# Hybrid decoder trunk on one core: the last weight unit of every expert layer packed by column halves, the output combined between the halves, and TensorE's branch placed at a fixed slot of a fetch block

## The reference, cut to what matters

```python
for layer in range(4):
    kind = layer % 3                     # 0 forgetting attention, 1 HGRN2, 2 short convolution
    mixed = (forgetting_attention, hgrn2, short_conv)[kind](x, ...)
    x = layer_norm(DEEPNORM_ALPHA * x + mixed, ln_mix_g[layer], ln_mix_b[layer])
    # 4 groups of 8 experts: the best group of each token, the two best experts in it
    gates = ...                          # (256 tokens, 32 experts), two non-zero values a token
    hg, hu = jnp.einsum('btd,edf->btef', x, w_gate), jnp.einsum('btd,edf->btef', x, w_up)
    h = jax.nn.silu(hg) * hu * gates[..., None]
    ffn = jnp.einsum('btef,efd->btd', h, w_down)
    x = layer_norm(DEEPNORM_ALPHA * x + ffn, ln_ffn_g[layer], ln_ffn_b[layer])
```

## Time and profile before

| | |
|---|---|
| median of 3 runs | 1457.16 us (1450.97 to 1460.29) |
| the profiled execution's own time | 1457.11 us |
| its span, first to last instruction | 1455.2 us |
| TensorE busy (matmuls / weight loads) | 90% / 50% of the span |
| VectorE, ScalarE, GpSimd busy | 25%, 21%, 7% |
| moved by DMA | 482 MB, 331 GB/s over the span |
| TensorE's mean granted clock | 0.987 of full speed |

### The profile page before, as it was taken

How to read it: one execution, slowest core, us unless ns; L and a number is a source line. 1 busy time by engine, 2 the same in 40 slices (tenths; PEclk the granted TensorE clock), 3 DMA queues, 4 the chain that set the end, 5 groups by cost and what they waited for, 6 DMA issues and landing times.

```text
span 1455.2 us, 18373 instructions
## 1 busy us (share of the span) xinstructions
PE 1308.8 (90%) x7662; PEld 734.2 (50%) x7662; DVE 364.8 (25%) x928; ACT 305.8 (21%) x751; POOL 96.4 (7%) x170
## 2 busy tenths in 40 slices
PE   8999988878999999888789999889789999888885
PEld 7855633422564865343328866333328765543331
DVE  1442311102615843111111133110112451311103
ACT  0241312112223312222111003221110251312210
POOL 2221000000001520000000000000001030000000
PEclk9999999999999999999999999999999999999998
DMA  9756699999735029999998837999998355899995
GB/s 320 278 225 274 257 427 429 426 427 415 311 122 225 2 84 422 429 426 429 427 427 355 370 144 275 428 427 427 428 417 360 118 231 235 331 428 426 429 426 212
DMA packets 36773, 481.97 MB, mean 331 GB/s; under 512 B 4416, under 2 KB 4736, under 8 KB 6864
## 3 DMA queue, kind: packets, MB, share of 16 engines
q1 hardware_dynamic: 35424, 478.19, 79.7%
q0 software_dynamic: 1120, 2.09, 0.7%
q10 hardware_dynamic: 144, 0.46, 0.1%
HBM read 479.60 MB, written 1.05 MB: 330 GB/s over the span
## 4 chain that ended last, share of the span: by engine, by line
PE 75%; DMA 13%; DVE 5%; ACT 4%; issue 2%; POOL 1%; SPq 0%; DVEq 0%; POOLq 0%
PE psum L785 15%; DMA memory<-in_units 13%; PE psum L1085 12%; PE psum L816 8%; PE psum L1045 8%; PE psum L844 8%; PE psum L1128 7%; PE psum L1120 7%; ACT memory L1224 2%; PE psum L824 1%; DVE memory L1912 1%; PE psum L1181 1%; ACT memory L1420 1%; PE psum L750 1%; PE psum L958 1%
## 5 line engine op out<-in xcount | busy, mean ns | idle before, releaser
L785 PE MATMUL psum<-memory,ring 128*128 128x256 f32 x1024 | 224.1, 382 | 1.5 <-DMA ring<-in_units 1.1
L785 PEld LDWEIGHTS psum<-memory,ring 128*128 128x128 f32 x1024 | 195.6, 191 | 29.0 <-issue 1.3
L1128 PE MATMUL psum<-memory 128*128 128x512 f32 x256 | 128.5, 628 | 42.8 <-DVE memory L1912 22.8
L1045 PE MATMUL psum<-memory,x 128*128 128x128 f32 x1024 | 130.6, 281 | 35.0 <-ACT memory L1224 35.0
L1045 PEld LDWEIGHTS psum<-memory,x 128*128 128x128 f32 x1024 | 119.3, 192 | 72.9 <-issue 69.9
L1085 PE MATMUL psum<-ring,memory 128*32 128x512 f32 x1152 | 136.2, 612 | 14.2 <-DMA ring<-in_units 14.0
L1224 ACT ACTIVATE memory<-psum,affine_t 128x128 f32<-128x128 f32 x312 | 117.3, 457 | 136.9 <-PE psum L1045 129.4
L1907 DVE TENSOR_TENSOR memory<-memory,psum 128x256 f32<-128x256 f32 x32 | 13.5, 421 | 461.9 <-ACT memory L1414 461.9
L844 PE MATMUL psum<-ring,memory 128*128 128x512 f32 x256 | 112.4, 594 | 1.4 <-DVE memory L1501 0.9
L1128 PEld LDWEIGHTS psum<-memory 128*128 128x128 f32 x256 | 44.7, 193 | 131.9 <-DVE memory L1912 48.2
L1085 PE MATMUL psum<-memory 128*32 128x512 f32 x896 | 103.5, 602 | 5.6 <-DMA memory<-in_units 5.5
(11 more groups left out here) (222 smaller groups left out, 1147.5 us busy)
## 6 DMA issues: line engine op xcount, KB each, us to landing
ring<-in_units SPq DMA_DIRECT2D x129, 2048.0 KB, 25.4
memory<-in_units SPq DMA_DIRECT2D x88, 2048.0 KB, 26.3
memory<-in_units SPq DMA_DIRECT2D x16, 1024.0 KB, 27.4
ring<-in_units SPq DMA_DIRECT2D x4, 512.0 KB, 10.5
memory<-in_const SPq DMA_DIRECT2D x3, 448.0 KB, 31.2
x<-in_x SPq DMA_DIRECT2D x2, 512.0 KB, 4.8
out<-x SPq DMA_DIRECT2D x2, 512.0 KB, 2.7
memory<-in_tables SPq DMA_DIRECT2D x1, 640.0 KB, 31.4
```

The costliest lines, as they stand in the source:

```text
L785: last = nc.tensor.matmul(bank(key, T, s * T), w[:, 2 * m + s, k, :], xT[:, k, :], start=(k == 0), stop=(k == KD - 1))
L1045: last = nc.tensor.matmul(psum[:, to, (at + i) * P:(at + i + 1) * P], x[:, c, k * P:(k + 1) * P], sel[:, par, c, :], start=(c == 0), stop= ...
L1128: last = nc.tensor.matmul(psum[:, 4 + NH * c + h, :], hT[:, FC + c, :], y_sb[:, h * HB:(h + 1) * HB], start=False, stop=last_quad, skip_gr ...
```

## The change

1. Packing: a second copy of each layer's last unit is added behind the others, laid out by output columns: columns 512 to 767 for both j first, then columns 768 to 1023. The last unit is loaded from this copy, in the same two DMAs of 1 MB.
2. `down(1)` of a last quad becomes `down_columns(0)` and `down_columns(1)`, of 256 columns each over both j, into bank 3 and bank 1. Each is eight matmuls, where each j of `down(1)` was four.
3. `combine(0)` moves between them, ahead of the wait on the second DMA. `combine(1)` becomes `combine_columns(0)` and `combine_columns(1)`, of 256 columns each; `z_ready` comes from the second.
4. ScalarE copies the two banks separately (128x256 each), the first once `columns_used` tells that `down_columns(0)` is done.
5. TensorE's flag read gets an alignment: it is put at slot 128 of a block of 256 instruction slots, and a branch leads over the padding.

```diff
+                    at = PACKED + unit[1]
                     for j in range(FC):
                         cols = slice(j * UNIT // FC, (j + 1) * UNIT // FC)
...
-                        if j and h == NH - 1 and last_quad and sems is first:
-                            pe.wait_ge(half_in, 16 * (n // NQ + 1))
...
-                if last_quad:
+                half = HB // 2
+                def down_columns(b):
+                    w = slots[GU + 1][0].rearrange("p (b j e c) -> p b e j c", b=2, e=QE, j=FC)
+                    for j in range(FC):
+                        for e in range(QE):
+                            rows = slice(W * e, W * (e + 1))
+                            last = nc.tensor.matmul(psum[rows, (3, 1)[b], 0:half], hT[:, j, rows], w[:, b, e, j],
+                                                    start=(j == 0), stop=(j == FC - 1))
+                    return last
+
+                def combine_columns(b):
+                    cols = slice(b * half, (b + 1) * half)
+                    return [nc.tensor.matmul(psum[:, 4 + NH * c + 1, cols], hT[:, FC + c, :], y_sb[:, HB:D][:, cols],
+                                             start=False, stop=True, skip_group_check=True) for c in range(TC)]
+
+                if last_quad and sems is first:
+                    l = n // NQ
+                    down(0)
+                    pe.wait_ge(*slots[GU + 1][1])
+                    down_columns(0).then_inc(columns_used, 1)
+                    combine(0)
+                    pe.wait_ge(half_in, 16 * (l + 1))
+                    down_columns(1).then_inc(sems["unit_used"], 1)
+                    pe.wait_ge(columns_ready, l + 1)
+                    combine_columns(0)
+                    pe.wait_ge(sems["y1_ready"], n + (1 + FREE))
+                    for last in combine_columns(1):
+                        last.then_inc(z_ready, 1)
+                elif last_quad:
...
                 experts(l)
+
+                pe.addr_align(256, offset=128, max_nops=0)
                 runs = more_path(pe, l, runs, experts_more)
...
+                if by_columns:
+                    act.wait_ge(columns_used, l + 1)
+                    nc.scalar.activation(y_sb[:, HB:HB + HB // 2], psum[:, 3, 0:HB // 2], ACT.Copy).then_inc(columns_ready, 1)
+                    act.wait_ge(sems["unit_used"], n * QU + QU)
+                    nc.scalar.activation(y_sb[:, HB + HB // 2:D], psum[:, 1, 0:HB // 2], ACT.Copy).then_inc(sems["y1_ready"], 1)
...
-    units = np.empty((PACKED, P, UNIT), np.float32)
+    units = np.empty((PACKED + DEPTH, P, UNIT), np.float32)
...
+        units[PACKED + l] = moe[-1, -1].reshape(P, FC, QE, 2, HB // 2).transpose(0, 3, 1, 2, 4).reshape(P, UNIT)
```

More of the change, by code:

```diff
@@ L428, in build @@
         unit_used, half_ready = sem("unit_used"), sem("half_ready")
+        columns_used, columns_ready = sem("columns_used"), sem("columns_ready")
         pair_gathered, pair_ready = sem("pair_gathered"), sem("pair_ready")
@@ L1129, in combine @@
                                                 start=False, stop=last_quad, skip_group_check=True)
-                        if last_quad and sems is first and h == NH - 1:
-                            last.then_inc(z_ready, 1)
                     if last_quad and sems is first and h == 0:
@@ L1409, in first_tokens, with quad @@
                 token_blocks(l, 0, (2, 3), 2).then_inc(first["xw_ready"], 1)
-            def quad(l, sems, n, par, ahead):
+            def quad(l, sems, n, par, ahead, by_columns=False):
                 act.wait_ge(sems["unit_used"], n * QU + (GU + spare(sems)))
@@ L1417, in quad @@
                     tokens(l, sems, n + 1, 1 - par, 1)
-                act.wait_ge(sems["unit_used"], n * QU + (QU + spare(sems)))
-                nc.scalar.activation(y_sb[:, HB:D], psum[:, 3, :], ACT.Copy).then_inc(sems["y1_ready"], 1)
+                if by_columns:
[3 more added lines that the diff above has]
+                    nc.scalar.activation(y_sb[:, HB + HB // 2:D], psum[:, 1, 0:HB // 2], ACT.Copy).then_inc(sems["y1_ready"], 1)
+                else:
+                    act.wait_ge(sems["unit_used"], n * QU + (QU + spare(sems)))
+                    nc.scalar.activation(y_sb[:, HB:D], psum[:, 3, :], ACT.Copy).then_inc(sems["y1_ready"], 1)
             def experts(l):
@@ L1428, in experts @@
                 for par in range(2):
-                    quad(l, first, l * NQ + NQ - 2 + par, par, par == 0)
+                    quad(l, first, l * NQ + NQ - 2 + par, par, par == 0, par == 1)
             def experts_more(l, runs):
```

## The result

Twelve runs of each: 1465.39 us median after (1461.18 to 1467.63), 1455.55 before (1450.97 to 1460.29). Ratio 1.0063, 95% interval 1.0051 to 1.0075 (the two medians alone give 1.0068). The profiled execution took 1461.18 us with a span of 1459.4; it is the fastest of its twelve, so it shows less of the loss (4.1 us) than the medians (9.8).

The account below looks back on a forecast made before the run. The weight stream was taken to bound the four expert ends, where matmuls wait for the last unit. 1457.11 us less 7.0 of gain plus 0.9 for the branch gave 1451.0 us, range 1445 to 1462.

Parts of the forecast that it names:

- the price of the branch: TensorE's branch after the flag read, layers 1 and 2: waits for a missing instruction block, 0.9 us lost together.
- the lower price: Branch in layers 1 and 2: transfer starts at once on landing, costing 0.4 and 0.5 us.
- The 2.46 us: Layer 1 of the kernel before: an instruction block is usable some 2.46 us after its transfer begins.
- The upper bound, 6.3: Branch in layers 1 and 2: transfer starts 4 us after landing, TensorE resumes 6.3 us after landing.
- L: Each layer's expert end: start of the first matmul of the last unit's second half, which waited for its DMA.
- the upper price: Branch in layers 1 and 2: late transfer, keep_busy at half clock, 5 us lost in each against before.
- the second case: Rival, chance 0.30: the branch over two blocks stalls TensorE in layers 1 and 2, sum 1457 to 1462 us.
- 5.1 us of gain in layers 0 and 3: Expert ends of layers 0 and 3: gains of 2.5 and 2.6 us, set against the stall's losses.
- The sum from L to the statistics: Expert ends: work before VectorE's first statistics on the second 512 columns falls to 2.66 us; layer 1 had 4.30.
- The cover before L: DMA wait in the expert ends: combine(0), 1.72 us, fits in layers 0 and 3, ends late in 1 and 2.
- My 7.0: Four expert ends: gains of 2.5, 0.5, 1.4 and 2.6 us, sum 7.0 us, bounds 5.2 and 8.3.
- Does the rest follow?: Stages behind the statistics: the gain is handed on whole; with a full stream, only layer 3's 2 to 3 us.

Follow-up runs that it names:

- columns_far: Changed kernel with the flag read aligned to slot 240 instead of 128 in layers 1 and 2: 1466.83 us, ratio 1.0089 to the kernel before.
- columns_only: Changed kernel without the alignment of the flag read: 1450.82 us, ratio 0.9967 to the kernel before.
- rows_between: Kernel before with only combine(0) moved between the two row halves of down(1), no column halves, no alignment: 1450.05 us, ratio 0.9975.
- align_only: Kernel before with only the alignment of the flag read to slot 128 added: 1455.40 us, ratio 1.0003.
- after_again: Changed kernel, unedited, measured again on the chip of three other runs: 1466.10 us, ratio 1.0081 to the kernel before.
- rows_overshoot: Kernel before, no column halves, flag read aligned to slots 128, 88, 80, 128 so layers 1 and 2 overshoot: 1467.54 us, ratio 1.0081.
- columns_fit: Changed kernel with the flag read aligned to slots 128, 160, 208, 128 of layers 0 to 3: 1459.61 us, ratio 1.0030 to the kernel before.
- busy_first: Changed kernel with the three keep_busy matmuls between padding and flag read instead of behind the branch: 1457.22 us, ratio 1.0022 to the kernel before.
- columns_unmoved: Column halves without alignment, combine(0) left behind both halves (edited from columns_only): 1456.22 us, ratio 1.0011 to the kernel before.
- early_overshoot: columns_only with an overshooting padding at the start of the last quads of layers 1 and 2: 1450.31 us, ratio 0.9975 to the kernel before.
- columns_busy_first: columns_only with the three keep_busy matmuls ahead of the flag read: 1448.85 us, ratio 0.9959 to the kernel before.

## Why the prediction was wrong

Forecast 1451.0 us in 1445 to 1462, measured 1465.39.

**The step that failed** is the price of the branch: "I take the lower price, the one that rows measure." The 2.46 us were the time from a transfer's start to its use, and the sum took the transfer to start with the landing. It started 3.3 us after it in layer 1 and 3.6 in layer 2; landing to use was 6.1 and 6.4 us by the same reckoning. The upper bound, 6.3, was the right value, and the trace before had the row for it: the branches of its layers 1 and 2 jump into a block too, and the next transfer begins 3.8 and 3.9 us after they end. Here is the first of the two transfers, in the 0.2 us from 765.6; its branch had ended at 761.93:

```profile
q8 instruction: 1, 0.02, 31.8%
```

The forecast used such a pass as no more than an upper end. The choice between the ends was made by the row that measured one piece of the wait, not the whole.

There is a row that speaks for a quick start, and the forecast didn't use it either. In layers 1 and 2 of the kernel before, the sequencer runs into a block in order, 17 and 13 slots ahead of the flag read by the count and so behind the wait at L; the next transfer began there at most 1.5 and 1.4 us after L (at 759.47 and 1084.57). In layer 2 of columns_far, 20 slots ahead, it began 3.3 us after L. So 3.3 us isn't what every entry costs under the stream; in all landings in a new block by a jump under it, in all kernels, it was 3.1 to 4.4. What sets the difference no run here shows.

**The case itself was right.** The slot count held in every layer: overshoot in 1 and 2, none in 0. It held for the further kernels too: each branch of over 2 us stood where the target's block was missing by the count, those of layer 3 among them, and none stood elsewhere. `keep_busy` at half clock behind the wait, estimated at 4.3 us, took 4.4 and 5.1. But with the upper price the second case read 1462, and the measurement is 3 us past that. Its losses were right in size (transposes at L + 13, against 12.5 to 13.9), but it set 5.1 us of gain in layers 0 and 3 against them, and these came to some 2 us together, as far as the clock is left out of it (below). The chance, 0.30, was too small for a case whose premises but one, the late start, stood in counts and in the rows that the forecast used.

**The sum from L to the statistics.** 2.66 us forecast, 2.60 to 2.67 in all four layers of all kernels with both parts, whatever the stream or the clock did before. The parts were right too: 0.99 us for the narrow half, ScalarE's copy hidden, VectorE's statistics out of the way. One reading beside it was wrong: the matmuls queued behind ScalarE's copy in the kernel before, from 759.70 to 762.50, are 2.8 us and not 3.4; nothing in the sum hangs on it.

**The cover before L.** I had expected `combine(0)` to end 1.1 us late in layer 1, 0.2 us late in layer 2 and not at all in layers 0 and 3. The trace has the time at which the second DMA reports (`half_in` is raised), and in every layer of the kernel before, L stands 0.04 us behind it. In the first profile of the changed kernel it stands 0.12, 0.49, 0.47 and 1.32 us behind. In layer 1 `combine(0)` is fed back to back between the first half, at 751.59, and L, 2.91 us in all, while the halves land 1083.21 - 1080.73 = 2.48 us apart, which is 1 MB at the 425 GB/s of the earlier trace rows. So there L is no longer the DMA's but TensorE's. Layer 3 loses more because the granted clock was at its lower level while `down(0)` ran ahead of the first half (layer 1, then layer 3, then the clock there):

```profile
749.20 1.92 PE L1119 MATMUL psum<-ring,memory 128*32 128x512 f32 x16 [1.10 <-DMA ring<-in_units]
...
1438.80 3.39 PE L1119 MATMUL psum<-ring,memory 128*32 128x512 f32 x16 [2.73 <-DMA ring<-in_units]
...
1438.80:1441.80 3.00, 3.00 (x16) 0.88 (x20) 0.00 (x0) 0.00 (x0) 0.00 (x0) 0.50 0.74 309
```

Such stretches stand ahead of L in most profiles, those of the kernel before among them. There they don't move L; with `combine(0)` in the cover, L was 1.2 to 1.5 us late behind most of them (2.3 once, 0.6 or less in others). Forecast and first expectation both took the cover at full clock.

From L the transposes come 7.84 - 6.16 = 1.68 us earlier at full clock, and the last layer ends 1.6 us earlier. In columns_only L was 0.09, 0.47, 0.04 and 1.34 us behind the arrival of the second half: 4.9 us gained in all, 4.6 measured by the medians (4.8 by the ratio, interval 2.6 to 7.1). For rows_between the same reckoning gives 4.0 us, 3.6 by the ratio. My 7.0 was too high, because it also booked the half-clock stretches of layers 0 and 3 of one execution: in align_only layer 3 was at L + 4.30 without any edit to this end. They come in some executions and not in others.

**Does the rest follow?** Yes, nearly. Take the time from the arrival of the second half (`half_in`) to the transposes, in layer 3 to the end of the program, add the four, and compare with align_only, the kernel before with full clock in all four (39.8 us). The last column is the ratio of all executions, in us; after and after_again are the changed kernel.

| kernel | four ends of its profile, against align_only | by the ratio (95%) |
|---|---|---|
| after | +9.1 us | +9.2 (7.4 to 10.9) |
| after_again | +11.8 | +11.8 (8.7 to 14.8) |
| rows_overshoot | +8.9 | +11.8 (8.3 to 15.3) |
| columns_far | +11.8 | +13.0 (10.8 to 15.1) |
| columns_fit | +4.9 | +4.4 (2.0 to 6.7) |
| busy_first | +1.5 | +3.2 (1.2 to 5.4) |
| columns_unmoved | +1.8 | +1.6 (-0.1 to 3.3) |
| early_overshoot | -2.8 | -3.6 (-5.5 to -1.9) |
| rows_between | -4.0 | -3.6 (-5.2 to -2.0) |
| columns_only | -4.9 | -4.8 (-7.1 to -2.6) |
| columns_busy_first | -3.5 | -6.0 (-7.9 to -4.1) |

So the four ends, stall and late L together, account for the time of every kernel within its interval but the last, whose profile is of the slowest of its twelve executions.

**What stays open.** The one profile of before is no full-clock one: its ends stand 3.2 us above align_only's, by the half-clock stretches in layers 0 and 3, so a part of its executions has a longer base than the table's. And a profile varies outside the ends. L of layer 0 comes at 348.8 us in the first profile of the changed kernel and at 355.3 in that of columns_only, which run the same code up to there. The first profile's loss, 4.1 us, is so small because before's profile has those 3.2 us in its ends and because layer 0's second half arrived 1.2 us later in it. From the transposes to the arrival of the next layer's second half, three layers together, the kernels that stall take 1060.5 to 1065.1 us, the others 1059.0 to 1062.8. One profile a kernel doesn't settle whether the stall adds something there or this is the DMA stream's own spread.

## What to carry to other kernels

Placing an instruction at a fixed slot of a fetch block is a promise about the code ahead of it: where the next one of its kind comes a few slots too late, the padding leads into a fresh block and a far branch behind it wants the one after, which here cost some 6 us from landing to use and put the transposes up to 7.8 us later than in the same kernel without the padding. Count the slots modulo the block for every instance, look at the branch's target and at what runs on from there to the block's end, and put work that fills time ahead of an instruction that may wait, not behind it. When a wait's two bounds lie far apart, take the row that measures the whole of it, from the event that starts it.

## What the runs showed of the hardware

- With the weight stream at 425 to 430 GB/s, the block behind the one into which TensorE's sequencer had jumped over padding was usable 5.7 to 6.6 us after the landing (eight landings in after, after_again, rows_overshoot and busy_first; 6.1 and 6.4 in the first profile). The transfer started 3.2 to 3.9 us after the landing, and the branch ended 2.5 to 2.9 us after that start.
- With the stream idle, at the end of layer 3, five such overshoots took 3.1 to 3.6 us from the landing to the end of the branch (3.1 in the changed kernel; the branch itself reads 2.3 to 2.9). The transfer started 0.7 to 1.3 us after the landing and was usable 2.3 to 2.8 us after its start. So it is above all the start that is late under the stream.
- An entry in order had its next transfer begin at most 1.5 and 1.4 us behind it in layers 1 and 2 of the kernel before, under the same stream, where the entry's place is by the slot count; in columns_far, layer 2, it was some 3.3 us.
- A branch that had to call for a block itself waited 6.3 and 7.1 us under the stream (columns_far) and 3.3 without it (layer 3 of columns_only).
- TensorE's branch to a block that was there took 0.31 to 0.47 us (the longest in layer 0 of rows_between), the short one over padding 0.17 to 0.20 us within a block and 0.28 to 0.39 into the next; ScalarE's took 45 to 54 ns.
- Behind 3.7 us of idle time the granted clock was still at its upper level in layer 2 of rows_overshoot; behind 5.3 us, in layer 1 of the changed kernel, it was at the lower.
